# Depthwise convolution beside a dense layer: fewer taps early, lower halves a unit sooner, last three slices in one turn

## The reference, cut to what matters

```python
def conformer_conv(h, w_pw1, b_pw1, w_dw, b_dw, ln_g, ln_b, w_pw2, b_pw2):
    a, gate = jnp.split(h @ w_pw1 + b_pw1, 2, axis=-1)
    y = a * jax.nn.sigmoid(gate)
    y = lax.conv_general_dilated(y, w_dw[:, None, :], window_strides=(1,),
                                 padding=[(CONV_K // 2, CONV_K // 2)],
                                 dimension_numbers=('NWC', 'WIO', 'NWC'),
                                 feature_group_count=CONV_W) + b_dw
    y = jax.nn.silu(layernorm(y, ln_g, ln_b))
    return y @ w_pw2 + b_pw2
```

## Time and profile before

| | us |
|---|---|
| median of 3 executions | 1522.09 |
| lowest, highest | 1521.91, 1522.61 |
| the profiled execution, its own time | 1522.05 |
| its span | 1520.7 |
| TensorE busy in the span | 1374.4 |
| VectorE busy in the span | 1188.6 |

### The profile page before, as it was taken

One profiled execution on the slowest core, in us unless ns is written; L12 is line 12 of the kernel. 1 busy time (PEld: TensorE's weight loads), 2 busy tenths in 40 slices (PEclk: granted clock), 3 DMA queues, 4 the chain that ended last, 5 costly groups with the idle time before them and its releaser, 6 DMA issues.

```text
span 1520.7 us, 20247 instructions
## 1 busy us (share of the span) xinstructions
PE 1374.4 (90%) x7310; PEld 1006.7 (66%) x7310; DVE 1188.6 (78%) x2402; ACT 720.7 (47%) x1636; POOL 341.6 (22%) x312
## 2 busy tenths in 40 slices
PE   8999999999999999999999999998787687877776
PEld 3878899999897999999888855444332232322222
DVE  6977888887998689897787787778877777767645
ACT  4555565456476755556354444333433343333322
POOL 1100100001000100003001354444644354434440
PEclk9999999999999999999999999999999899999999
DMA  9764369998530489994433699999999999999995
GB/s 388 316 243 161 144 224 357 361 351 312 208 126 1 167 330 369 349 343 160 167 111 139 238 422 422 420 422 421 420 422 421 422 421 421 422 422 421 422 421 243
DMA packets 66341, 477.12 MB, mean 314 GB/s; under 512 B 7361, under 2 KB 7361, under 8 KB 9153
## 3 DMA queue, kind: packets, MB, share of 16 engines
q0 software_dynamic: 36864, 268.45, 42.5%
q1 hardware_dynamic: 29376, 207.37, 36.5%
q10 hardware_dynamic: 2, 0.01, 0.0%
HBM read 474.75 MB, written 1.05 MB: 313 GB/s over the span
## 4 chain that ended last, share of the span: by engine, by line
PE 52%; DMA 30%; DVE 10%; ACT 4%; issue 2%; POOL 1%; ACTq 0%; DVEq 0%; POOLq 0%
DMA ring<-in_uv,crow 11%; DMA row_x<-in_uv,crow 9%; PE ps L2344 7%; PE ps L1896 5%; PE ps L1897 5%; PE ps L1898 5%; DMA HID<-in_uv,crow 5%; PE ps L2213 3%; DMA ring<-in_um 3%; PE ps L2216 3%; PE ps L2215 3%; PE ps L2240 3%; PE ps L2357 2%; DVE WB L537 2%; PE ps L1929 2%
## 5 line engine op out<-in xcount | busy, mean ns | idle before, releaser
L537 DVE TENSOR_TENSOR WB<-ring,WB 128x1024 fp32r<-128x1024 f32 x208 | 256.0, 1233 | 46.7 <-ACT WB L1366 44.6
L1366 ACT ACTIVATE WB<-ring 128x1024 fp32r<-128x1024 f32 x208 | 218.5, 1052 | 120.4 <-PE ps L2216 87.0
L1896 PE MATMUL ps<-hH,WB 128*128 128x256 f32 x752 | 216.1, 287 | 5.3 <-DVE WB L537 3.3
L2344 PE MATMUL ps<-ring,P 128*128 128x512 f32 x376 | 175.1, 611 | 46.0 <-ACT P L1727 46.0
L1898 PE MATMUL ps<-hH,WB 128*128 128x256 f32 x752 | 213.4, 284 | 0.0
L1897 PE MATMUL ps<-hL,WB 128*128 128x256 f32 x752 | 213.3, 284 | 0.0
L1717 ACT ACTIVATE On<-On 128x2 f32<-128x2 f32 x126 | 25.6, 203 | 358.7 <-DVE On L1282 358.6
L522 DVE CUSTOM_DVE_ANT_0 ring<-ring,crow,cols 128x1024 f32<-128x1024 f32 x128 | 163.7, 1281 | 20.0 <-DMA ring<-in_um 19.8
L2344 PEld LDWEIGHTS ps<-ring,P 128*128 128x128 f32 x376 | 69.7, 193 | 149.3 <-ACT P L1727 77.2
L1282 DVE CUSTOM_DVE_ANT_0 ring<-ring,cT 128x1024 f32<-128x1024 f32 x94 | 114.5, 1225 | 62.9 <-DMA ring<-in_uv,crow 62.2
L1896 PEld LDWEIGHTS ps<-hH,WB 128*128 128x128 f32 x752 | 144.7, 192 | 7.9 <-DVE WB L537 4.3
(11 more groups left out here) (353 smaller groups left out, 2899.1 us busy)
## 6 DMA issues: line engine op xcount, KB each, us to landing
ring<-in_stream SPq DMA_DIRECT2D x112, 1024.0 KB, 6.1
ring<-in_um SPq DMA_DIRECT2D x66, 1024.0 KB, 7.5
ring<-in_wm SPq DMA_DIRECT2D x4, 1024.0 KB, 12.8
bias<-in_bias SPq DMA_DIRECT2D x2, 2048.0 KB, 15.4
HID<-in_um SPq DMA_DIRECT2D x4, 512.0 KB, 18.3
row_h<-in_stream SPq DMA_DIRECT2D x2, 1024.0 KB, 8.0
ring<-in_uv,crow POOLq DMA_INDIRECT x94, 27.5
xT<-in_xT SPq DMA_DIRECT2D x1, 1024.0 KB, 8.9
```

The costliest lines, as they stand in the source:

```text
L537: ve.tensor_tensor(unit_dst(j, 1), unit_src(j), f(unit_dst(j, 0)), ALU.subtract).then_inc(s_lo, 1)
L1366: se.activation(unit_dst(j, 0), unit_src(j), ACT.Copy).then_inc(s_hi, 1)
L1896: te.matmul(o, wh[:, c], hi[:, kt, :], start=(kt == 0), stop=False)
L2344: mm = te.matmul(ps[4 + 2 * n + q][:, :], diag[:, g % 8, :], row_ap[row_of[g]][:, 1024 + q * 512:1536 + q * 512], start=(g % 128 == 0), st ...
```

## The change

It has four parts. `pump` allows three open slices once two slices are done. The pumping behind the units goes from 4 taps to 2 for units 0 to 6 (4 from unit 7 on), and between the two halves of a unit's taps stands one more `ahead`, which writes one lower half earlier (of unit 5 ahead of the second tap at all, and from there one unit sooner than before, up to the same last unit). The means of slices 3 and 4 are both put last, so five stand between the taps and three behind. And ScalarE's table load with the upper half behind it moves from behind the last emptying to behind the last diagonal. VectorE also waits for slice 3 before it centres.

```diff
+            def running():
+                return {kt for kt, _ in chains}
+
             def pump(n):
                 for _ in range(n):
                     for kt in CV:
-                        if len(chains) < 2 and kt not in begun and kt in given:
+                        if len(chains) < (3 if len(begun - running()) > 1 else 2) and kt not in begun and kt in given:
                             begun.add(kt)
-                            chains.append(taps(kt))
+                            chains.append((kt, taps(kt)))
                     if not chains:
                         return
                     c = chains.pop(0)
-                    if next(c):
+                    if next(c[1]):
                         chains.append(c)
...
                     unit(first["pw1", s] + u)
-                    if (s, u) == (0, 1):
-                        pump(2)
-                        ahead(raw_at["conv"] + 3)
-                        pump(2)
-                    else:
-                        pump(4)
+                    j = 4 * s + u
+                    pump(1 if j < 7 else 2)
+                    if j:
+                        ahead(first["pw1", 0] + min(15, j + (2 if j < 3 else 1)))
+                    pump(1 if j < 7 else 2)
             pump(200)
             V.wait_ge(s_mean, 1)
             V.wait_ge(*y_v[CV[-1]])
+            V.wait_ge(*y_v[CV[-2]])
...
             for d in range(len(TAPS) + 8):
+                if d == len(TAPS):
+                    sqrt_next()
+                    ahead(first["pw2", 0])
                 if d >= 8:
...
-            sqrt_next()
-            ahead(first["pw2", 0])
...
-            means = CV[:-1] + CP + CV[-1:]
+            means = CV[:-2] + CP + CV[-2:]
...
-                if kt == CP[-1] and 14 <= k < 20:
+                if kt == CP[-1] and 14 <= k < 19:
                     mean_product(means[k - 14])
-            for kt in means[6:]:
+            for kt in means[5:]:
                 mm = mean_product(kt)
```

## The result

The changed kernel takes 1525.26 us, the median of 14 executions (1522.51 to 1528.62), and the kernel before, run as often beside it, 1521.91 us (1520.18 to 1524.28). The ratio is 1.0022, with a 95% interval of 1.0014 to 1.003: 3.3 us slower, between 2.1 and 4.6. The forecast was 1525.4.

The account below looks back on a forecast made before the run. TensorE was taken as the bound up to 473.7, with VectorE finishing within a microsecond. Terms: 1.25 later at the last tap, +0.43 third mean product, -0.75 table, +2.35 clock, +3.3 in all: 1525.4 us, range 1522.7 to 1526.6.

Parts of the forecast that it names:

- VectorE's taps end at 471.35, slice 2's at 467.4: Layer 1's convolution: VectorE's last tap 3.2 us sooner than 474.55; slice 2 ends ten taps earlier, before near 456.
- The count of lone intervals, 26 x 0.124: VectorE's taps: 26 intervals of a slice alone, each 0.124 us dearer, go, saving 3.2 us.
- TensorE's first tap at 425.9: After the weight units: first tap 4.8 us sooner than 430.7, 3.1 of the hole and 1.7 of half clock.
- A stall of 6.5 us at the third mean: TensorE, due at slice 2's mean at 460.9, idles until slice 2 ends at 467.4.
- One more product behind the emptying, 0.43: Behind the last tap: three mean products stand there instead of two, costing 0.43 us more.
- The table, -0.75: ScalarE's table load and split, covered by TensorE's taps, let products of squares follow the centring 0.75 us sooner.
- Wait, third mean and table together +0.95: Products of squares start at 478.0 against 477.06, 0.95 us later, before any clock loss.
- The clock, 2.35, ends 1.7 and 3.0: TensorE's products behind the stall run at half clock, costing 2.35 us, with forecast ends 1.7 and 3.0.
- VectorE's end decides: Rival: slice 2's mean is no wait, centring at 472.0, 1517.9 us; needs slice 2 done before 460.9; chance 0.12.
- The clock holds: Rival: no half clock behind the stall, or it is back in time; only +0.95 stays, 1523.0 us; chance 0.10.
- The lower halves make VectorE wait: Rival: sooner lower halves wait for ScalarE's upper halves, slice 2 and all behind 1.8 later, 1527.2 us; chance 0.06.
- slower by more than 0.2%: Whole kernel: time above 1525.1 us, given a chance of 0.51.

Follow-up runs that it names:

- mean2_last: The changed kernel with slice 2's mean product also put behind the last tap; 1518.47 us, ratio 0.9976 against the kernel before.
- two_open: The changed kernel with at most two slices open, as before; 1522.56 us, ratio 1.0005 against the kernel before.
- old_units: The changed kernel with four taps behind every unit and the lower halves as before; 1520.99 us, ratio 0.9995 against the kernel before.
- table_only: The kernel before with only ScalarE's table load and upper half moved ahead of the last emptying; 1521.56 us, ratio 1.0002.
- fill_stall: The changed kernel with seven stand-in products into a free bank ahead of the third mean's wait; 1523.1 us, ratio 1.0005 against the kernel before.
- three_only: The kernel before with only the three open slices, units, order of means and table as before; 1529.37 us, ratio 1.0052.

## Why the prediction was right, point by point

The forecast held in its mechanism and nearly in its size. Its own steps, on the clock of before (0.95 taken off the trace of the change):

- *VectorE's taps end at 471.35, slice 2's at 467.4.* They ended at 471.27, and TensorE was released at 467.37. The count of lone intervals, 26 x 0.124, was the right one.
- *TensorE's first tap at 425.9.* It came at 426.1 (427.1 in the trace), at full clock and without the hole. The gain was 4.6 us and not 4.8 and, as forecast, worth nothing, since all of it went into waiting.
- *A stall of 6.5 us at the third mean.* It was 6.12. mean2_last removes it by moving one product, two_open by having slice 2 ready, and old_units by bringing TensorE late enough.
- *One more product behind the emptying, 0.43.* The last row of the means has six records in 1.56 us where the earlier trace rows had four in 1.13.
- *The table, -0.75.* table_only shows -0.67.
- *Wait, third mean and table together +0.95.* fill_stall shows +1.08.
- *The clock, 2.35, ends 1.7 and 3.0.* It was 1.75 in the profile, and 1.66 by the difference to fill_stall: at the lower end, that of the earlier trace rows's first stretch, after an idle half as long. This is the one term that was off; the middle of two rows was a choice, and the row whose work was alike (dense products) was the nearer one. With 1.75 the sum is +2.7, and +2.74 is what the trace has. The term also stood on less than it seemed: behind an idle of 2.9 us in the same place the clock fell in the profiles of before and old_units and held in those of three_only and table_only. The clock behind the new stall was seen in one execution; the times fit it, with fill_stall 2.2 us faster than the change by the medians.

The times say 3.3 us (2.1 to 4.6), which holds both 2.7 and the forecast. That the point fell within 0.2 us of the median is luck in part: the clock term was 0.6 too high, and the median lies 0.6 above the sum that the trace gives. The two profiled executions differ by only 2.22, because 0.95 came ahead of the stage and some 1.2 were given back in the second MLP: the first update behind the convolution (L999, L1002) starts at 492.19 and 495.89, the last update of the second MLP (L886) at 699.6 and 702.1. I did not find a cause in the change for that; the same stretch took 3.0 us more in the profile of fill_stall than in that of before (L886 at 704.1, L1002 at 493.68), so it differs between executions by more than the effect.

Of the rivals, *VectorE's end decides* was the state that mean2_last then made, at 472.1 for the centring as worked out; it fell for the change because its condition, slice 2 done before 460.9, was missed by 6.5 us. *The clock holds* is what fill_stall made by hand; by itself the clock held only behind the shorter idle near 400. *The lower halves make VectorE wait* fell: of the idle times forecast there only the 0.27 us ahead of unit 5's lower half occurred, and it was in the sum. That the change was slower by more than 0.2% was given half the chance, and the measured 0.22% lies at that line, too.

## What to carry to other kernels

Where an in-order engine waits for another's results one by one, the order of these waits has to be the order in which the results get ready, and an edit that shares turns more evenly moves each of them: here it made the last one 3 us sooner and slice 2 eleven us later. So after such an edit, write down for every consumer when its input is now done and when the consumer arrives; here the arrival had moved 4.6 us ahead and the input 11 us back, and one product in the wrong place cost more than the whole edit could gain. An engine freed early is not a gain by itself: it idles, and after TensorE's idles of 4 us and more here, part of the idle time was charged again as slow products behind it (1.75 us in the change).

## What the runs showed of the hardware

- After TensorE's idle times of 4.21, 5.42 and 6.12 us the granted clock was 0.5, and 4.9, 3.1 and 3.5 us behind it passed at that level (two_open, three_only, the change); the idle of 6.45 us among the products of the second half had 5.9 us behind it. Among the first three the loss did not grow with the length of the idle time. I had taken it to.
- After the idle of 2.9 us near 400, with the same products around it, the outcome varied between profiles: 3.4 us at 0.5 in before and in old_units, none in three_only and table_only. So one profile doesn't tell what such an idle costs.
- An idle of 1.00 us (mean2_last) and the 0.65 us ahead of the last means left the clock at 1.00.
- A table load on ScalarE took 1.28 us in every profile, and the dummy root came 1.29 to 1.30 us behind the start of its load (474.58 and 475.88 in the change); the drain of 1.38 us that the prediction weighed does not show beside it.
